# A two-layer decoder trunk with eight experts: expert weight units hold u and g in turn, and the final norm is written twice

## The reference

```python
def rmsnorm(x, g):
    xf = xf * lax.rsqrt(jnp.mean(xf * xf, axis=-1, keepdims=True) + EPS)
    return xf.astype(x.dtype) * g

def swiglu(x, w13, w2):                 # w13: 1024 x 7168 of an expert, w2: 3584 x 1024
    g, u = jnp.split(x @ w13, 2, axis=-1)
    return (jax.nn.silu(g) * u) @ w2

def moe_swiglu(xn, router_w, w13, w2):  # top 2 of 8 experts for each token
    ...
    for e in range(N_EXPERTS):
        out = out + gates[:, e:e + 1] * swiglu(xt, w13[e], w2[e])
```

## Time and profile before

| | |
|---|---|
| Runs | 1345.71 us median (1344.3 to 1346.89) |
| Profiled execution | own time 1345.04 us, span 1343.2 us |
| TensorE busy | 1321.8 us, 98% |
| VectorE, ScalarE busy | 408.6 us (30%), 331.0 us (25%) |
| DMA, mean | 444.57 MB, 331 GB/s |
| Granted TensorE clock, mean | 0.998 |

### The profile page before, as it was taken

How to read it: one execution, slowest core, us unless ns; L and a number is a source line. 1 busy time by engine, 2 the same in 40 slices (tenths; PEclk the granted TensorE clock), 3 DMA queues, 4 the chain that set the end, 5 groups by cost and what they waited for, 6 DMA issues and landing times.

```text
span 1343.2 us, 29602 instructions
## 1 busy us (share of the span) xinstructions
PE 1321.8 (98%) x13165; PEld 1047.9 (78%) x13165; DVE 408.6 (30%) x773; ACT 331.0 (25%) x616; POOL 14.8 (1%) x28
## 2 busy tenths in 40 slices
PE   9999999999999999998999999999999999999996
PEld 6989888888798989654988898666898666898652
DVE  6686764444758754000101100101100100100101
ACT  6565554443646542000001000000000000000001
POOL 1100000000000000000000000000000000000000
PEclk9999999999999999999999999999999999999999
DMA  8935355555544679999999999999999999999995
GB/s 315 341 135 215 99 195 189 188 189 188 181 155 152 240 305 396 380 420 420 420 420 419 420 410 364 411 421 420 419 421 418 421 420 421 419 418 420 420 421 213
DMA packets 63931, 444.57 MB, mean 331 GB/s; under 512 B 7293, under 2 KB 8717, under 8 KB 10936
## 3 DMA queue, kind: packets, MB, share of 16 engines
q1 hardware_dynamic: 61976, 437.22, 81.4%
q0 software_dynamic: 1824, 5.42, 1.2%
HBM read 441.17 MB, written 1.44 MB: 330 GB/s over the span
## 4 chain that ended last, share of the span: by engine, by line
PE 90%; DMA 4%; SPq 3%; DVE 2%; issue 1%; ACT 1%; DVEq 0%; ACTq 0%
PE bank L2079 49%; PE bank L1637 10%; PE bank L1639 10%; PE bank L1638 10%; SPq L495 3%; PE bank L2031 2%; DMA slot_w_hi<-in_moe_units 2%; DMA slot_xT_lo<-in_moe_units 2%; PE bank L2145 2%; PE bank L1732 1%; PE bank L1679 1%; DVE w_lo L977 1%; PE bank L2056 1%; PE bank L2057 1%; PE bank L1867 1%
## 5 line engine op out<-in xcount | busy, mean ns | idle before, releaser
L977 DVE TENSOR_TENSOR w_lo<-raw,w_hi 128x1024 fp32r<-128x1024 f32 x154 | 181.6, 1219 | 42.3 <-ACT w_hi L617 41.5
L1547 DVE TENSOR_TENSOR hidden<-hidden,bank 128x384 f32<-128x384 f32 (+1 forms) x56 | 27.3, 488 | 545.7 <-ACT hidden L921 545.7
L617 ACT ACTIVATE w_hi<-raw 128x1024 fp32r<-128x1024 f32 x154 | 155.1, 1058 | 47.7 <-PE bank L1639 47.6
L921 ACT ACTIVATE hidden<-bank 128x384 f32<-128x384 f32 (+1 forms) x56 | 24.5, 438 | 395.0 <-PE bank L2079 395.0
L2079 PE MATMUL bank<-raw,mid_x 128*32 128x128 f32 (+1 forms) x1680 | 97.4, 380 | 0.0
L2079 PEld LDWEIGHTS bank<-raw,mid_x 128*32 128x32 f32 x1680 | 93.4, 110 | 3.3 <-issue 2.8
L912 ACT ACTIVATE hT<-bank 128x384 f32<-128x384 f32 (+1 forms) x56 | 24.5, 438 | 287.0 <-PE bank L2145 287.0
L1637 PE MATMUL bank<-xT_hi,w_hi 128*128 128x256 f32 x320 | 91.6, 286 | 0.0
L1638 PE MATMUL bank<-xT_lo,w_hi 128*128 128x256 f32 x320 | 90.5, 283 | 0.0
L1639 PE MATMUL bank<-xT_hi,w_lo 128*128 128x256 f32 x320 | 90.5, 283 | 0.0
L2079 PE MATMUL bank<-raw,hT 128*32 128x256 f32 (+2 forms) x760 | 88.2, 486 | 1.8 <-DMA raw<-in_moe_units 1.7
(11 more groups left out here) (340 smaller groups left out, 2037.5 us busy)
## 6 DMA issues: line engine op xcount, KB each, us to landing
raw<-in_moe_units SPq DMA_DIRECT2D x109, 1024.0 KB, 23.8
slot_w_hi<-in_moe_units SPq DMA_DIRECT2D x47, 1024.0 KB, 23.1
slot_w_lo<-in_moe_units SPq DMA_DIRECT2D x46, 1024.0 KB, 23.1
raw<-in_layer_units SPq DMA_DIRECT2D x44, 1024.0 KB, 5.3
raw<-in_dense_units SPq DMA_DIRECT2D x33, 1024.0 KB, 5.2
slot_bias<-in_moe_units SPq DMA_DIRECT2D x19, 1024.0 KB, 23.0
slot_xT_lo<-in_moe_units SPq DMA_DIRECT2D x19, 1024.0 KB, 23.8
slot_qk<-in_moe_units SPq DMA_DIRECT2D x18, 1024.0 KB, 22.7
```

The lines of the kernel that those rows point to most:

```text
L617: act.activation(w_hi[:, st.split(u), half, :], raw[:, st.slot(u), half * n:(half + 1) * n], ACT.Copy)\
L921: act.activation(hidden[:, 0:n * P], bank[2][:, 0:n * P], ACT.Silu).then_inc(sem("silu"), 1)
L977: dve.tensor_tensor(w_lo[:, st.split(u), half, :], raw[:, st.slot(u), half * n:(half + 1) * n], w_hi[:, st.split(u), half, :].bitcast(F32) ...
L1547: dve.tensor_tensor(hidden[:, 0:n * P], hidden[:, 0:n * P], bank[j % 2][:, 0:n * P], ALU.mult)\
```

## The change

An expert unit of the up weights now holds two k blocks by 1024 columns: u and g of the same 512 hidden columns in turn, 128 by 128. One up phase of a step reads four such units; u and g of a block lie side by side in banks 0 and 1, declared as one tensor. `turn_hidden(j - 1)` and what hangs behind it stand in front of `up(j)`. The final norm's code is called in an `If(n_items < NE + 1)` ahead of the overflow code and again behind the loop in it. The second half of the second tile's output is computed by ScalarE, from a fifth bank that holds (x + y) times gain. The root's refinement has three VectorE operations in place of four, with one more small operation ahead of it.

```diff
+def expert_units(w13, w2):
+    def ups(j):
+        cols = [c + j * FT + b * P + np.arange(P) for b in range(FT // P) for c in (FE, 0)]
+        both = w13[:, np.concatenate(cols)]
+        return [unit(both, 2 * m, 2, 0, 2 * FT) for m in range(KD // 2)]
+    out = ups(0)
+    for j in range(1, ITEM_STEPS):
+        out += ups(j) + down_blocks(w2, j - 1)
+    return np.stack(out + down_blocks(w2, ITEM_STEPS - 1))
...
+    up_banks = ctx.enter_context(nc.psum_tensor("up_banks", [P, 1024], F32))
+    bank = [up_banks[:, 0:512], up_banks[:, 512:1024]]
...
+    def ups_of(n, gate):
+        return up_banks[:, 0:2 * n * P].rearrange("p (b s c) -> p b s c", b=n, s=2)[:, :, gate, :]
...
-                act.activation(hidden[:, 0:n * P], bank[2][:, 0:n * P], ACT.Silu).then_inc(sem("silu"), 1)
+                act.activation(hidden_of(n), ups_of(n, 1), ACT.Silu).then_inc(sem("silu"), 1)
...
+        def last_norm():
+            m = 3 * DEPTH + 1
+            for t in range(NT):
+                for half in range(2):
+                    act.wait_ge(sem("last_out_mm"), 2 * t + half + 1)
+                    act.activation((spare, v)[t][:, half, :], bank[last_banks[2 * t + half]][:, :], ACT.Square,
+                                   accum_out=ss[:, t, half:half + 1]).then_inc(sem("square"), 1)
+                guess(m, t)
+            act.wait_ge(sem("last_rstd"), 2)
+            act.wait_ge(sem("last_out_mm"), 5)
+            act.activation(xn[:, 1, 512:1024], bank[weighed_bank][:, :], ACT.Copy, scale=rstd[:, 1:2])\
+                .then_inc(sem("last_piece"), 1)
+        with act.If(n_items < NE + 1):
+            last_norm()
         with act.If(n_items > NE):
...
-            c.step(dve.tensor_scalar(mean[:, a], ss[:, t, 1:2], 1.0 / D, half_mean[:, a], ALU.mult, ALU.add))
+            c.step(dve.tensor_scalar(neg_mean[:, a], ss[:, t, 1:2], -0.5 / D, half_neg[:, a], ALU.mult, ALU.add))
...
-            c.link(dve.scalar_tensor_tensor(newton[:, a], mean[:, a], r0[:, a], r0[:, a], ALU.mult, ALU.mult))
-            c.link(dve.tensor_scalar(newton[:, a], newton[:, a], -0.5, 1.5, ALU.mult, ALU.add))
-            last = dve.tensor_tensor(rstd[:, a], r0[:, a], newton[:, a], ALU.mult)
+            c.link(dve.scalar_tensor_tensor(newton[:, a], neg_mean[:, a], r0[:, a], r0[:, a], ALU.mult, ALU.mult))
+            last = dve.scalar_tensor_tensor(rstd[:, a], newton[:, a], 1.5, r0[:, a], ALU.add, ALU.mult)
...
-            dve.tensor_tensor(hidden[:, 0:n * P], hidden[:, 0:n * P], bank[j % 2][:, 0:n * P], ALU.mult)\
+            dve.tensor_tensor(hidden_of(n), hidden_of(n), ups_of(n, 0), ALU.mult)\
...
+        dve.wait_ge(sem("last_y"), 1)
+        dve.tensor_tensor(weighed_y[r, :], last_y[r, :], g_row[r, 512:1024], ALU.mult).then_inc(sem("weighed_y"), 1)
         half_means(m, 0)
-        root(m, 0)
+        root(m, 0, "last_rstd")
+        dve.wait_ge(sem("last_rstd"), 1)
+        last_scaled(0, 0)
         half_means(m, 1)
-        last_scaled(m, 0)
-        root(m, 1)
-        last_scaled(m, 1)
+        last_scaled(0, 1)
+        root(m, 1, "last_rstd")
+        dve.wait_ge(sem("last_rstd"), 2)
+        last_scaled(1, 0)
...
+        def few_up(w, k, start, stop):
+            a = (k % 2) * 1024
+            for half in range(2):
+                mm = product(bank[0][half * FEW:(half + 1) * FEW, :], few_x[:, k, :], w[:, a + half * 512:a + (half + 1) * 512],
+                             start, stop)
...
+        def mid_up(w, k, start, stop):
+            a = (k % 2) * 1024
+            rows = [mid_x[:, k, g * 32:(g + 1) * 32] for g in range(3)]
             for g in range(3):
+                product(bank[0][g * 32:(g + 1) * 32, :], rows[g], w[:, a:a + 512], start, stop)
+            for g in range(2):
+                product(bank[0][96:128, g * 256:(g + 1) * 256], rows[g], w[:, a + 768:a + 1024], start and g == 0, stop)
             for g in range(3):
+                product(bank[1][g * 32:(g + 1) * 32, 0:256], rows[g], w[:, a + 512:a + 768], start, stop)
+            return product(bank[1][96:128, 0:256], rows[2], w[:, a + 768:a + 1024], start, stop)
...
+            def up(j):
+                for m in range(KD // 2):
+                    if m == 2 and j == 0 and first_rows:
                         pe.wait_ge(sem("rows_in"), 2)
+                    w = arrived((6 * j - 2 if j else 0) + m)
+                    for k in range(2 * m, 2 * m + 2):
+                        mm = one_up(w, k, k == 0, k == KD - 1)
                     mm.then_inc(sem("units_read"), 1)
...
             for j in range(begin + 1, end):
-                e = 6 * j - 2
-                up(e, j % 2, j - 1)
-                up(e + 2, 2)
+                turn_hidden(j - 1)
+                if between is not None:
+                    between(j)
+                up(j)
                 pe.wait_ge(sem("turned"), steps_done(i, j - 1))
                 down(j - 1, 0)
...
+                elif j == ITEM_STEPS and i == NE - 1:
+                    lay_weighed_x(1)
...
+        with pe.If(n_items < NE + 1):
+            last_return()
         with pe.If(n_items > NE):
```

More of the change, by code:

```diff
@@ L158, in weight_blocks @@
     w13, w2 = given["w13_moe"][0], given["w2_moe"][0]
-    blocks["moe_units"] = np.concatenate([swiglu_units(w13[e], w2[e], FE) for e in range(NE)])
+    blocks["moe_units"] = np.concatenate([expert_units(w13[e], w2[e]) for e in range(NE)])
     return blocks
@@ L399, in _build @@
     place8 = pool_b[:, 1, 0:NT * NE].rearrange("p (t e) -> p t e", t=NT)
-    mean, half_mean, lnv, r0, newton, rstd = (norm_s[:, i, :] for i in range(6))
+    neg_mean, half_mean, lnv, r0, newton, rstd, half_neg = (norm_s[:, i, :] for i in range(7))
     router_wide = pool_inv[:, :, :].rearrange("p b t -> p (b t)")
@@ L457, in _build @@
     last_banks = (6, 7, 1, 5)
+    weighed_bank = 0
     xlogit_banks = (2, 3, 6, 7)
@@ L557, in _ @@
         sp.nop()
-        for t in range(NT):
-            for half in range(2):
-                s = slice(half * 512, (half + 1) * 512)
-                sp.wait_ge(sem("xn_ready"), 4 * (3 * DEPTH + 1) + 2 * t + half + 1)
-                sp.dma_start(io["out"][0, t * P:(t + 1) * P, s], xn[:, t, s]).then_inc(sem("out_done"), 16)
+        for n in range(2 * NT):
+            t, s = n // 2, slice(n % 2 * 512, (n % 2 + 1) * 512)
+            sp.wait_ge(sem("out_ready" if n < 3 else "last_piece"), n % 3 + 1)
+            sp.dma_start(io["out"][0, t * P:(t + 1) * P, s], xn[:, t, s]).then_inc(sem("out_done"), 16)
         sp.wait_ge(sem("out_done"), 32 * NT)
@@ L1526, in sums_lo, with weigh_x @@
             last.then_inc(sem("y_sb"), 1)
-        def last_scaled(m, t):
-            dve.wait_ge(sem("gain_in"), 16 * m)
-            for half in range(2):
-                s = slice(half * 512, (half + 1) * 512)
-                dve.scalar_tensor_tensor(xn[:, t, s], bank[last_banks[2 * t + half]][:, :], rstd[:, t:t + 1], g_row[:, s],
-                                         ALU.mult, ALU.mult).then_inc(sem("xn_ready"), 1)
+        def weigh_x():
+            dve.tensor_tensor(weighed_x[:, :], x[:, 1, 512:1024], g_row[:, 512:1024], ALU.mult).then_inc(sem("weighed_x"), 1)
         def add_back(i, col, which):
@@ L2047, in lay_x, with lay_weighed_x @@
                           skip_group_check=True)
+        def lay_weighed_x(times):
+            pe.wait_ge(sem("weighed_x"), times)
+            pe.matmul(bank[weighed_bank][:, :], ident, weighed_x[:, :], start=True, stop=False, skip_group_check=True)
         def lay_out(i):
@@ L2227, in between, with last_return @@
                     lay_x()
+                elif j == ITEM_STEPS and i == NE - 1:
+                    lay_weighed_x(1)
             item(i, item_units(i), many, between)
+        def last_return():
+            pe.wait_ge(sem("last_y"), 1)
+            for n, b in enumerate(last_banks):
+                t, half = n // 2, n % 2
+                r = slice(half * FEW, (half + 1) * FEW)
+                pe.matmul(bank[b][:, :], spread[r, half, t * P:(t + 1) * P].bitcast(F32), last_y[r, :], start=False, stop=True,
+                          skip_group_check=True).then_inc(sem("last_out_mm"), 1)
+            pe.wait_ge(sem("weighed_y"), 1)
+            r = slice(FEW, 2 * FEW)
+            pe.matmul(bank[weighed_bank][:, :], spread[r, 1, P:2 * P].bitcast(F32), weighed_y[r, :], start=False, stop=True,
+                      skip_group_check=True).then_inc(sem("last_out_mm"), 1)
+        with pe.If(n_items < NE + 1):
+            last_return()
         with pe.If(n_items > NE):
@@ L2245, in _ @@
             lay_x()
+            lay_weighed_x(2)
+            last_return()
         pe.nop()
-        pe.wait_ge(sem("last_y"), 1)
-        for n, b in enumerate(last_banks):
-            t, half = n // 2, n % 2
-            r = slice(half * FEW, (half + 1) * FEW)
-            pe.matmul(bank[b][:, :], spread[r, half, t * P:(t + 1) * P].bitcast(F32), last_y[r, :], start=False, stop=True,
```

(1 more changed line is left out.)

71 lines of the change are left out of this document (28 added, 43 removed).

## The result

The changed kernel takes 1347.49 us (median of 22 runs, 1346.26 to 1349.1) against 1345.26 us (22 runs, 1343.72 to 1346.89): ratio 1.0018, 95% interval 1.0011 to 1.0024, so 2.2 us slower where 6.6 were forecast. At 0.18% the change also lies within the 0.2% that the prediction calls no change, an outcome to which it gave 9%. The profiled execution has 1346.36 us of its own and a span of 1344.3, against 1343.2 before: +1.1.

The account below looks back on a forecast made before the run. TensorE and DMA were both taken as full in the expert stage, with 2.07 us of TensorE room. 1.35 + 8.85 - 1.2 + 0.90 - 2.07 - 1.25 = +6.6 us gave 1351.8 us, own range 1348.5 to 1355, 8 in 10 1347 to 1357.

Parts of the forecast that it names:

- What would show it: Signs: 1 to 1.5 us idle before transposes once per item, 96-row up units at 2.58, 0.2 us behind last_y.
- So a 96-row up unit saves 0.: Expert stage, 96-row items: the new up unit still takes 2.58 us, as a down unit of that form does; bound -1.6.
- Waits, 8.85: Transposes at an item's first turn wait for silu and product: 4 x 1.35 + 3 x 1.15 us behind 632.57.
- Head, 1.35: Item 0's first wait, where DMA is starved, makes the landing at 632.57 come 1.35 us later.
- 64-row pace, -1.2: Items 3, 5, 7: an up unit takes 1.715 in place of 1.73 us, over 28 units each, -1.2 us.
- Fifth piece, 0.90, and room, -2.07: One more 512-column matmul on TensorE costs 0.90 us; TensorE's three late landing waits hide 2.07 us of added work.
- Root in the layers, 0: The other norms lose a 0.15 us instruction each beside a busy TensorE: 0, at most -1 us.
- End, -1.25: After last_y: -0.8 us from TensorE's avoided jump, -0.45 from shorter roots and ScalarE's last piece.
- where the outgoing DMA covers them: At the end: ScalarE's and TensorE's jumps, now behind their last work, are hidden by the outgoing DMA.
- Rival A: DMA keeps the bound in the expert stage, so added waits count only where DMA runs short: +1.8, 1347 us; 9%.
- Rival B: Products cost by their number: a 96-row up unit falls to 36 records, 1.94 us; -7, 1338 us; 6%.
- Rival C: The waits before transposes are long, at upper bounds 2.2 and 1.95 us: 16.9 in place of 10.2, 1358 us; 10%.

Follow-up runs that it names:

- turn_front: The kernel before with the transposes of step j-1 moved in front of both up units, products unchanged: 1351.66 us.
- quarter_first: The kernel before with the fourth column quarter's three small products ahead of the three large ones in each k block: 1348.95 us.
- items_only: The kernel before with only the change's expert stage (unit layout, products, transposes in front); norms, end and last piece as before: 1346.79 us.
- room6: The kernel before with six unused products of 512 columns on TensorE at step 5 of item 7, ahead of the last landings: 1347.08 us.
- straight_end: The changed kernel without the overflow items' code on TensorE and ScalarE, so nothing is jumped over: 1346.40 us.
- old_root: The changed kernel with the old root refinement of four small VectorE operations: 1348.45 us.
- filled: The changed kernel with returned rows, places and gather put ahead of the transposes at an item's first turn: 1342.63 us.
- front_copy: The kernel before with the last return and last squares copied in front of the overflow items' code: 1344.58 us.

## Why the size was wrong

All that "What would show it" names came (the 0.2 us behind last_y as 0.04), and none of its signs of being wrong: the mechanism of the waits is right. The 4.4 us between forecast and measurement are in the sizes of its terms, and 3.1 of them in one. Point by point, by the steps of the forecast:

- **"So a 96-row up unit saves 0."** This step failed. The unit does take 2.58 as before; what was missed is what it leaves behind. Under the old products the unit in front of transposes takes 2.87, under the new 2.75, at 26 steps behind the landing: -3.1 us. The prediction met this once, in the wait ("a down-shaped last unit ends a little earlier, I take 1.35" in place of 1.4), and did not carry it to the transposes of all the other steps. The items show it directly. From start to start, item 0's second part grew by 0.63 (86.89 to 87.52) and item 2 by 0.39 (120.53 to 120.92), where the wait alone is 1.22: 0.59 over five steps, 0.83 over seven. The lower bound of the step, -1.6, did not hold it either, as it was put on the up units and not on the turn. turn_front and quarter_first show that it comes from the form and order of the up products. The records fit a fourth quarter of the array that runs behind: in turn_front three records of the next unit (660.01) start before the last one of the up unit (660.08), and that one is 128 columns wide, the form of the fourth quarter's products. In the kernel before it is the same between an up and a down unit, in the changed kernel no record does this. That is read from records, not isolated by a run, and quarter_first, which was to cure it by order, made it worse (2.96). Why the difference is 0.12 is open. The records of the kernel before:

```profile
656.85 0.60 PE L2079 MATMUL bank<-slot_w_hi,hT 128*32 128x512 f32 x3
656.88 0.27 PE L2079 MATMUL bank<-slot_xT_hi,mid_x 128*32 128x128 f32 x1
```

- **Waits, 8.85.** Place, number and releaser right; too long by 1.0: 4 x 1.22 + 3 x 1.00 = 7.9. Of the first wait the timeline after, which answers to the earlier trace rows, shows a part of why: the product ends at 525.39 and TensorE starts 0.06 later, where I took the 0.15 of the earlier trace rows.

```profile
524.25 0.49 ACT L945 ACTIVATE hidden<-up_banks 128x384 f32<-128x384 f32 x1 [8.34 <-PE up_banks L2130]
...
524.84 0.55 DVE L1577 TENSOR_TENSOR hidden<-hidden,up_banks 128x384 f32<-128x384 f32 x1 [4.75 <-ACT hidden L945]
...
525.45 0.55 PE L2194 MATMUL bank<-mats,hidden 128*128 128x128 f32 x3 [1.24 <-DVE hidden L1577]
```

- **Head, 1.35.** In this pair 1.0; the four kernels with the old place and products have 117.41 to 118.23, mean 117.88, the six with the new ones 118.41 to 119.51, mean 118.94.
- **64-row pace, -1.2.** Item 3, with its wait of 1.00, grew by 0.71 (82.68 to 83.39): -0.29 an item, -0.9 in all.
- **Fifth piece, 0.90, and room, -2.07.** 0.82 by items_only and 2.28 by room6, with an uncertainty of half a microsecond in the latter.
- **Root in the layers, 0.** About -0.7, so a busy TensorE did not cover it; at which norms it counts was not traced.
- **End, -1.25.** -0.91. The jump's -0.8 is right in size (0.97 to 0.04). Of the -0.45 for root and piece nothing is left: without the fetch the two gain about 0.35 (10.27 in straight_end against 10.60 to 10.65 with the old pieces and root), nearly all of it the root's (the last piece is ready at 7.16 in the changed kernel, at 7.48 in old_root), and the fetch takes 0.34 of that back in this trace, up to 1.4 in others. The step that failed is "where the outgoing DMA covers them": the jumps, now behind the last work, read their page through the engines that carry the output.

Sum by measured terms: 1.0 + 7.9 - 3.1 - 0.9 + 0.8 - 2.3 - 0.7 - 0.9 = +1.8, against +2.2 in the medians and +1.1 between the two profiled executions. The Trainium skill ("Runtime: NRT & Kernel Launch", "Instruction fetch mechanics") says that a taken branch out of the current pages forces a DMA fetch before execution goes on. The trace agrees in the kernel before (0.97) and shows no stall in four others with the same jump (0.04). That the sequencer fetches there while TensorE still works is inferred from these gaps and from when the reads begin.

Rival A gave nearly the measured time by a wrong reason: it had the waits hidden by DMA, and they are all in the stage. Rival B is out: an up unit fell from 48 records to 36 and still takes 2.58. Rival C is out by the 1.22. Two figures of the prediction are off by its own rows and carry nothing: the expert stage (515 to 1331.6) is 61% of the span and not 57%, and rival B's dip of two slices is worth 5.3 us and not about 6.

## What to carry to other kernels

When a block of small products changes its form, compare not only its own time but that of the next product that needs the whole array. When a step is moved in front of the work that hid its input, look at what stands right behind it: here four products that depended on nothing were enough to cover the wait (filled), and the kernel became faster than before. Ask of a jump or fetch that is moved behind the last work what else is on the DMA engines then. A stall read at the end of a program has a condition, so ask what held the sequencer before costing its removal.

## What was not expected of the hardware

- The cost of products in 32-column groups carries over: 2.75, 2.87 or 2.96 us (quarter_first) for the unit ahead of a full-array product, by the form and order of products up to two units earlier, while units by themselves take 2.58 or 2.62.
- The same jump cost 0.93 us behind a landing that TensorE had waited for, and nothing on TensorE in four other kernels.
- One 16 KB read of instructions among the 1.05 MB of output goes with a median landing of 2.2 (front_copy) to 3.1 us in place of 2.0 to 2.1, and without the code that is jumped over there is neither.
- Between executions of the same code the stretch in which TensorE waits for DMA scatters by 1.1 us, the stretch behind it, where it never does, by 0.05.
